# Expert weights of a mixture-of-experts backbone: the out-blocks of the first round issued from GpSimd instead of SP

## The reference

```
logits = h @ router_w                       # (256 tokens, 8)
top_vals, top_idx = top_k(logits, 2);  gates = softmax(top_vals)
combine = sum over the two of one_hot(top_idx) * gate      # (256, 8)
for e in range(8):
    g, u = split(h @ w_in[e])               # w_in[e]:  1024 x 7168
    out += combine[:, e] * ((silu(g) * u) @ w_out[e])      # w_out[e]: 3584 x 1024
```

## Time and profile before

| | us |
|---|---|
| median of 3 runs | 1665.91 (1664.21 to 1666.26) |
| the profiled execution's own time | 1665.85 |
| its span, first to last instruction | 1664.1 |
| TensorE busy in the span | 1574.3 (95%) |
| VectorE / ScalarE / GpSimd busy | 520.9 / 393.8 / 34.5 |
| queue q1 (SP's DMAs) | 467.64 MB, 71.2% of 16 engines' span |
| queue q0 (GpSimd's DMAs) | 4.88 MB, 1.0% |

### The profile page before, as it was taken

One profiled execution on the slowest core, in us unless ns is written; L12 is line 12 of the kernel. 1 busy time (PEld: TensorE's weight loads), 2 busy tenths in 40 slices (PEclk: granted clock), 3 DMA queues, 4 the chain that ended last, 5 costly groups with the idle time before them and its releaser, 6 DMA issues. The chain is left out here.

```text
span 1664.1 us, 27554 instructions
## 1 busy us (share of the span) xinstructions
PE 1574.3 (95%) x12212; PEld 907.7 (55%) x12212; DVE 520.9 (31%) x810; ACT 393.8 (24%) x701; POOL 34.5 (2%) x70
## 2 busy tenths in 40 slices
PE   5999989999999989998899999999999989999887
PEld 2855678878788877866634343343433433334332
DVE  3427367665532366447601001020100200101013
ACT  3327442221232243339401000010100101001011
POOL 1000100010000000000000000000000000000000
PEclk8999999999999999999899999999999999999998
DMA  9661815576523423212698999999999999999995
GB/s 366 214 215 38 269 51 195 188 260 229 218 100 102 138 83 117 81 68 103 269 366 342 413 424 423 423 424 423 425 423 423 425 422 424 424 422 424 424 420 199
DMA packets 87292, 474.34 MB, mean 285 GB/s; under 512 B 9128, under 2 KB 33096, under 8 KB 50304
## 3 DMA queue, kind: packets, MB, share of 16 engines
q1 hardware_dynamic: 84096, 467.64, 71.2%
q0 software_dynamic: 3072, 4.88, 1.0%
HBM read 471.36 MB, written 1.13 MB: 284 GB/s over the span
## 5 line engine op out<-in xcount | busy, mean ns | idle before, releaser
L1184 PE MATMUL ps<-w_moe,h_te 128*32 128x512 f32 (+2 forms) x3776 | 371.0, 540 | 14.8 <-DMA w_moe<-in_expert_in_w_dram 14.8
L1184 PE MATMUL ps<-w_hi,h_t 128*128 128x512 f32 (+1 forms) x960 | 295.0, 388 | 11.5 <-DVE h_t L1867 5.4
L1184 PEld LDWEIGHTS ps<-w_moe,h_te 128*32 128x32 f32 x3776 | 119.3, 110 | 271.8 <-issue 246.7
L1184 PE MATMUL ps<-h_t,w_hi 128*128 128x512 f32 (+1 forms) x768 | 222.5, 375 | 6.2 <-DVE h_t L1867 6.2
L1184 PEld LDWEIGHTS ps<-w_hi,h_t 128*128 128x128 f32 x960 | 180.9, 191 | 49.4 <-DVE w_lo L1992 4.3
L2332 DVE TENSOR_TENSOR residual<-residual,ps 128x512 f32<-128x512 f32 x24 | 16.5, 688 | 599.2 <-PE ps L1184 599.2
L1809 DVE TENSOR_TENSOR w_lo<-w_raw,w_hi 128x2048 fp32r<-128x2048 f32 x57 | 130.5, 2291 | 228.2 <-ACT w_hi L784 227.7
L1184 PE MATMUL ps<-w_lo,h_t 128*128 128x512 f32 (+1 forms) x480 | 185.6, 387 | 0.0
L784 ACT ACTIVATE w_hi<-w_raw 128x2048 fp32r<-128x2048 f32 x57 | 108.9, 1912 | 301.5 <-PE ps L1184 301.5
L1184 PEld LDWEIGHTS ps<-h_t,w_hi 128*128 128x128 f32 x768 | 141.4, 191 | 33.9 <-issue 9.2
L1184 PE MATMUL ps<-w_moe,work 128*32 128x512 f32 (+1 forms) x1456 | 147.2, 529 | 3.3 <-DVE y_split L2307 3.2
(11 more groups left out here) (277 smaller groups left out, 1127.0 us busy)
## 6 DMA issues: line engine op xcount, KB each, us to landing
w_moe<-in_expert_in_w_dram SPq DMA_DIRECT2D x94, 1792.0 KB, 24.1
w_moe<-in_expert_out_w_dram SPq DMA_DIRECT2D x63, 1024.0 KB, 27.4
work<-in_expert_in_w_dram SPq DMA_DIRECT2D x34, 1792.0 KB, 26.5
w_raw<-in_ada_w_dram SPq DMA_DIRECT2D x48, 1024.0 KB, 5.4
work<-in_expert_out_w_dram SPq DMA_DIRECT2D x30, 1024.0 KB, 25.9
w_raw<-in_ffn_in_w_dram SPq DMA_DIRECT2D x44, 512.0 KB, 4.9
w_extra<-in_expert_out_w_dram SPq DMA_DIRECT2D x19, 1024.0 KB, 27.2
w_raw<-in_diff_qkv_w_dram SPq DMA_DIRECT2D x12, 1024.0 KB, 5.2
```

The costliest lines, as they stand in the source:

```text
L1184: return pe.matmul(out_, l, r, start=first, stop=last, skip_group_check=True)
```

## The change

GpSimd issues all out-blocks of the first round, SP only the in-blocks. Slots, order of use and sizes stay. GpSimd first waits for `order_rdy`, loads the 7 numbers, waits for what SP waited for before it fetched O 0, O 1 and O 2 of expert 0, issues these three, and then goes through the out-blocks of `FETCHES` with the same waits on `used`. An out-block is announced by one of 11 new semaphores `o_landed`, taken in turn, instead of its slot's; the fill counts of the slots count in-blocks only. Further rounds stay with SP.

```diff
+O_SEMS = 11
...
-    fills, count, fetches = {b: 1 for b in place}, [1] * (IN_SLOTS + OUT_SLOTS), []
+    fills, count, fetches = {b: 1 for b in place}, [1] * IN_SLOTS + [0] * OUT_SLOTS, []
...
-        count[s] += 1
+        count[s] += b[0] != "O"
...
     # SP, experts(0)
                 fetch(0, "G", 0, 2)
-                fetch(0, "O", 0, 0)
...
-                fetch(0, "O", 0, 1)
-                sp.wait_ge(hn_done, XT)
-                fetch(0, "O", 0, 2)
                 order = [0]
                 for (kind, e, i), after in FETCHES:
+                    if kind == "O":
+                        continue
...
     # GpSimd, after its last small DMA
+        pool.wait_ge(order_rdy, 1)
+        order = [0] + [pool.value_load(ORD[0:1, j:j + 1], min_val=0, max_val=NE - 1) for j in RANK_AT[1:]]
+
+        def fetch_out(e, i):
+            rows = expert_out_w[0, order[e], 256 * i:256 * i + 256, :].rearrange("(p j) n -> p j n", j=2)
+            pool.dma_start(moe_view(0, "O", e, i), rows).then_inc(o_landed[(14 * e + i) % O_SEMS], 16)
+
+        pool.wait_ge(scores, U0 + U1)
+        pool.wait_ge(used, B_MOE)
+        pool.wait_ge(hn_done, XT)
+        for i in range(OUT_SLOTS):
+            fetch_out(0, i)
+        for (kind, e, i), after in FETCHES:
+            if kind == "O":
+                pool.wait_ge(used, B_MOE + after)
+                fetch_out(e, i)
...
     # TensorE, weights(kind, e, i)
-                pe.wait_ge(w_landed[moe_slot(rnd, kind, e, i)], moe_landed(rnd, kind, e, i))
+                if rnd == 0 and kind == "O":
+                    pe.wait_ge(o_landed[(14 * e + i) % O_SEMS], 16 * ((14 * e + i) // O_SEMS + 1))
+                else:
+                    pe.wait_ge(w_landed[moe_slot(rnd, kind, e, i)], moe_landed(rnd, kind, e, i))
```

More of the change, by code:

```diff
@@ L360, in backbone @@
     landed = [sem(f"landed{i}") for i in range(RAW)]
-    w_landed = [sem(f"w_landed{i}") for i in range(IN_SLOTS + OUT_SLOTS)]
+    w_landed = [sem(f"w_landed{i}") for i in range(IN_SLOTS + LATER_OUT)]
+    o_landed = [sem(f"o_landed{i}") for i in range(O_SEMS)]
     hi_done = sem("hi_done")
```

## The result

The changed kernel takes 1674.5 us (median of 5 runs, 1671.42 to 1675.64) against 1665.48 us before (5 runs, 1664.21 to 1666.26): a ratio of 1.0048, 95% interval 1.0038 to 1.0059. It is slower by 9.0 us, as forecast; single executions lie up to 4.2 us apart, so that the median meets the forecast to the tenth is luck.

What follows compares the result with a forecast made beforehand. It took DMA and TensorE as both close to the bound, the end being the last in-block's landing plus 58.2 us. Terms 0 + 0 + 8.7 us on 1665.85 gave 1674.5 us, range 1664 to 1690.

Steps and rivals of the forecast that it cites:

- What bounds the kernel: Experts' part: DMA and TensorE both close to the bound; the end is the last in-block's landing plus 58.2 us.
- five blocks ahead: Upper end of the forecast case: five out-blocks landed before expert 7's U 7 without being needed yet, 1679 us.
- Issuing costs nothing: SP loses 112 issues, GpSimd gains 112 of about 0.55 us, hidden by the 25 us to landing: 0 us.
- The first three out-blocks cost nothing: Expert 0's first three out-blocks go out later, their 7.4 us of DMA mostly in a hole: 0 us.
- Two queues on the same engines, 3.5 x 2.47 = 8.7 us: At a 64 to 36 share, 3.5 out-blocks on average move ahead of the last in-block, delaying it 8.7 us.
- the offset: Out-blocks' lead counted for one expert only, three blocks, since queues shorten in 9 or 16 us without issues between experts.
- B: Rival: engines share by time, not by row; 7.5 blocks ahead, 18.5 us, 1684.4 us; chance 0.18.
- C: Rival: 8192-byte rows go as two 4 KB packets, out-queue starved at 22%; 22 us, 1687.9 us; chance 0.09.
- D: Rival: nothing; out-blocks build no queue or order is restored between experts; 0 to 2.5 us, 1667 us; chance 0.14.
- E: Rival: faster, as a second queue fills small holes and raises the rate to 430 GB/s; 1662.2 us; chance 0.12.

Runs made afterwards that it cites:

- the run dealt out in twos: Against the kernel before: list of fetches dealt out in twos, two blocks to SP, the next two to GpSimd, so both queues hold both kinds; 1672.29 us, ratio 1.0036.

## Why the prediction was right

*What bounds the kernel.* The end is the landing of the last in-block plus a constant: right. U 7's start moved by 8.55 us, the tail by 1.0, so it is constant to about a microsecond only. One reading was off: 836:901 moved 397 GB/s, not 418 to 424; and five blocks ahead give 1678.2 us, not 1679. The sum uses neither.

*Issuing costs nothing.* Right: GpSimd issues one out-block in 0.53 us, and with all blocks on it the time is that of before.

*The first three out-blocks cost nothing.* Right. They went out at 829.66 to 831, one or two us later than the forecast 827 to 829, the hole at 830:834 went from a share of 0.03 to 0.76, and moving them back changed nothing.

```profile
829.66 0.56 POOL L777 DMA_DIRECT2D work<-in_expert_out_w_dram  x1 [36.75 <-issue]
...
830.74 0.53 POOL L777 DMA_DIRECT2D w_extra<-in_expert_out_w_dram  x1
```

*Two queues on the same engines, 3.5 x 2.47 = 8.7 us.* Right in mechanism and size. The lead of expert 7 arises where the prediction puts it: when G 0, G 1 and G 2 have landed, 1, 2 and 3 out-blocks are ahead of need, and 3 remain through the pairs. Three out-blocks had landed before U 7, and the fourth was begun: from 1612.1 to 1614.5 at 36% of 424 GB/s are 0.37 MB, a third of it, so 3.3 x 2.47 = 8.2 us, where 8.55 were measured. When the experts' part begins, the changed run is already 0.47 us late (first matmul at 829.26 instead of 828.79), which fills the rest. That two microseconds with rows of other lengths sufficed to tell the share was luck. By the shares alone row for row and block for block can't be told apart, in those two microseconds or with the halved rows, so the sum didn't hang on it. The turns of the single packets, above, settle it: row for row.

*Why the offset does not grow.* I had argued that the queues shorten between experts. This is only part of it. They do at experts 4 and 6: when G 4 lands, no issued out-block is still on its way, and the lead falls from 4 blocks to 1 within the next three or four in-blocks. At expert 7 it does not fall. That nothing adds up over eight experts has the better reason that the engines never stand still: a block that came early doesn't come again. The prediction's three blocks hold for experts 5 and 7; at the others one or two whole ones were ahead of U 7.

*The waits.* Forecast 30 us, measured 25.9. The 4.3 us more are only half of the delay. A wait of 2.39 us at 1152.72 and one of 2.15 us at 1363.73 were each followed by a block that took 4.75 and 4.91 us instead of 3.21, the first of them with the granted clock at 0.57 in 1152:1156 (its level of 1.2 GHz is 0.50): 3.2 us of TensorE's time that count as busy. Together they are 7.5 of the 8.55 us. The first, with its clock:

```profile
1152.72 4.75 PE L1200 MATMUL ps<-w_moe,h_te 128*32 128x512 f32 x32 [2.39 <-DMA w_moe<-in_expert_in_w_dram]
...
1152.00:1156.00 4.00, 3.28 (x16) 0.79 (x20) 0.00 (x0) 0.00 (x0) 0.00 (x0) 0.57 1.00 423
```

*Rivals.* B (shares by time) and C (starved because rows are cut to 4 KB) fell with the packet counts and with the time. C's case came up in the run with halved out-blocks, at twice its price (47 instead of 22 us, some 8 of them the shorter rows). D fell with the interval. E: no stretch of the earlier trace rows came above 424 GB/s. The Trainium skill (DMA: Bandwidth & Descriptors, Issuing engines are not separate DMA queues) says that several issuers bring no bandwidth. The trace agrees: 422 GB/s from 912 to 1606 us before and after. The Trainium skill (DMA: Bandwidth & Descriptors, SWDGE vs HWDGE vs iDMA) prefers packets of at most 4096 bytes. That does not show here: 212 packets of q0 carried 1.52 MB, 7.2 KB each with the short ones that close a block. Longer rows than 4 KB on this queue were not new either: q0 carried 48 rows of 4608 and 4800 bytes before the change, which the prediction overlooked.

## What to carry to other kernels

When the DMA engines never stand still, moving transfers to a second queue moves no more bytes in the same time; it only changes the order. Here, with rows of 4 to 14 KB, the engines took the rows of two full queues in turn, so the ratio of the rows' lengths set the ratio of the queues. Look for the last transfer that the end hangs on, and count what would land before it without being needed: each such block costs its transfer time, once. Keep one queue in the order of need where a kernel is bound by its loads; a second one is harmless where its blocks are taken back before the end.

## What the runs showed of the hardware that I had not expected

GpSimd's queue alone keeps the engines as full as SP's: 423 to 424 GB/s from 1100 us on with all blocks on it. From 912 to 1100 it moved 407 instead of 418, since the hole of 907:912 lay at 912:917 (share 0.03) in that later execution; from 917 to 1100 it is 418 against 421.

Rows of 7168 or 4096 bytes instead of 14336 or 8192 lower the rate of one queue: from 1100 us on it is 418 to 420 GB/s instead of 423 or 424.

After the same wait of 3.24 to 3.25 us before the last expert's out-blocks, the first 32 matmuls took 5.29 us before, 6.38 in the change and, in the run dealt out in twos, 3.64:

```profile
1624.71 3.64 PE L1212 MATMUL ps<-w_moe,work 128*32 128x512 f32 x32 [3.25 <-DVE y_split L2339]
...
1624.70:1628.30 3.60, 3.59 (x33) 0.96 (x33) 0.16 (x1) 0.00 (x0) 0.00 (x0) 1.00 0.73 266
```

```profile
1628.20:1634.50 6.30, 6.30 (x33) 1.37 (x33) 0.12 (x1) 0.00 (x0) 0.53 (x1) 0.56 0.61 230
```

The second row of the first fence and the fence below it are the stretches of these matmuls: the granted clock was 1.00 in the one run and 0.56 in the other, so mostly at the level of 1.2 GHz. The end varies by up to 2.7 us between runs for this reason; why the clock fell in one run and not in the other, after the same wait, was not tried.
